# Odd layer of a two-block network: eight blocks of the output projection placed ahead of the last gate products

## The reference, cut to what matters

```python
def lru_direction(xc, w_a, b_a, w_x, b_x, lam, reverse):
    r = jax.nn.sigmoid((jnp.einsum('btnd,nde->btne', xb, w_a).reshape(B, T, W) + b_a).astype(jnp.float32))
    i = jax.nn.sigmoid((jnp.einsum('btnd,nde->btne', xb, w_x).reshape(B, T, W) + b_x).astype(jnp.float32))
    log_a = -LRU_C * r * jax.nn.softplus(-lam.astype(jnp.float32))
    a = jnp.exp(log_a)
    b = jnp.sqrt(-jnp.expm1(2.0 * log_a)) * i * xc.astype(jnp.float32)
    ...

def odd_layer(z, w_in, conv_w, conv_b, w_a, b_a, w_x, b_x, lam, w_out):
    zp = jnp.einsum('btd,de->bte', z, w_in)
    u, gate = split_cols(zp, ODD_SPLITS)
    ...
    y = (lru_direction(xc, w_a[0], b_a[0], w_x[0], b_x[0], lam[0], reverse=False)
         + lru_direction(xc, w_a[1], b_a[1], w_x[1], b_x[1], lam[1], reverse=True))
    y = y * jax.nn.silu(gate)
    return jnp.einsum('bte,ed->btd', y, w_out)
```

## Time and profile before

| what | value |
|---|---|
| median of 3 runs | 1892.74 us (1888.79 to 1895.13) |
| profiled execution | span 1893.4 us |
| TensorE busy | 1860.5 us, 98% of the span |
| VectorE, ScalarE, GpSimd busy | 606.7, 431.5 and 60.8 us |
| odd layer, from its first matmul on | 1687 to 1893 us of the span |
| output projection in the trace | 1833.4 to 1890.3 us |

### The profile page before, as it was taken

One profiled execution on the slowest core, in us unless ns is written; L12 is line 12 of the kernel. 1 busy time (PEld: TensorE's weight loads), 2 busy tenths in 40 slices (PEclk: granted clock), 3 DMA queues, 4 the chain that ended last, 5 costly groups with the idle time before them and its releaser, 6 DMA issues.

```text
span 1893.4 us, 20864 instructions
## 1 busy us (share of the span) xinstructions
PE 1860.5 (98%) x8529; PEld 1015.8 (54%) x8537; DVE 606.7 (32%) x1501; ACT 431.5 (23%) x954; POOL 60.8 (3%) x61
## 2 busy tenths in 40 slices
PE   9999999999999999999999999999999999999999
PEld 8888754443443433455444344433365657468864
DVE  3665433111110103135311111100434556424662
ACT  2322211100000101142110010000135434217760
POOL 0000000000000000000000000000010000001110
PEclk9999999999999999999999999999999999999999
DMA  9433459999999999416999999999731313231530
GB/s 385 193 131 141 156 203 375 424 427 428 429 428 429 428 429 426 179 54 252 398 422 430 427 430 427 427 429 428 332 114 45 134 45 134 107 121 40 222 122 34
DMA packets 42640, 529.40 MB, mean 280 GB/s; under 512 B 4592, under 2 KB 8208, under 8 KB 10544
## 3 DMA queue, kind: packets, MB, share of 16 engines
q1 hardware_dynamic: 39728, 515.39, 65.6%
q10 hardware_dynamic: 2816, 12.65, 1.7%
HBM read 523.80 MB, written 4.23 MB: 279 GB/s over the span
## 4 chain that ended last, share of the span: by engine, by line
PE 82%; DMA 7%; DVE 5%; issue 4%; ACT 2%; POOL 1%; ACTq 0%; DVEq 0%; POOLq 0%
PE ps L202 33%; PE ps L689 20%; PE ps L712 10%; PE ps L721 5%; PE ps L659 4%; DMA ring<-in_wu 3%; DMA ring<-in_wg 3%; PE ps L1355 1%; PE ps L654 1%; PE ps L571 1%; PE ps L698 1%; PE ps L497 1%; PE ps L988 1%; POOL small L2592 1%; PE ps L1137 0%
## 5 line engine op out<-in xcount | busy, mean ns | idle before, releaser
L689 PE MATMUL ps<-ring,work 128*64 128x512 f32 x1792 | 393.2, 593 | 3.3 <-DMA ring<-in_wu 1.8
L202 PE MATMUL ps<-xl,ring 128*128 128x256 f32 (+3 forms) x1344 | 292.3, 376 | 0.9 <-DVE xl L2305 0.9
L689 PEld LDWEIGHTS ps<-ring,work 128*64 128x64 f32 x1792 | 128.3, 137 | 260.1 <-issue 254.0
L202 PEld LDWEIGHTS ps<-xl,ring 128*128 128x128 f32 x1344 | 245.3, 191 | 40.3 <-issue 2.3
L202 PE MATMUL ps<-ring,xl 128*128 128x256 f32 (+2 forms) x672 | 202.8, 459 | 2.1 <-DVE work L2288 1.1
L712 PE MATMUL ps<-ring,work 128*64 128x512 f32 x896 | 199.3, 596 | 2.3 <-ACT work L1580 2.3
L202 PE MATMUL ps<-ring,big 128*128 128x512 f32 x448 | 197.9, 598 | 2.9 <-ACT ring L1859 2.4
L2153 DVE TENSOR_TENSOR work<-work,ps 128x512 f32<-128x512 f32 x32 | 22.0, 687 | 524.5 <-PE ps L689 524.5
L202 PEld LDWEIGHTS ps<-ring,xl 128*128 128x128 f32 x672 | 125.5, 190 | 70.1 <-issue 57.2
L202 PEld LDWEIGHTS ps<-ring,big 128*128 128x128 f32 x448 | 84.3, 191 | 105.2 <-issue 102.1
L712 PEld LDWEIGHTS ps<-ring,work 128*64 128x64 f32 x896 | 61.5, 137 | 117.5 <-issue 114.3
(11 more groups left out here) (374 smaller groups left out, 1671.3 us busy)
## 6 DMA issues: line engine op xcount, KB each, us to landing
ring<-in_wg SPq DMA_DIRECT2D x56, 2048.0 KB, 17.6
ring<-in_wu SPq DMA_DIRECT2D x56, 2048.0 KB, 20.5
ring<-in_wd SPq DMA_DIRECT2D x56, 2048.0 KB, 22.8
xl<-in_wg SPq DMA_DIRECT2D x8, 2048.0 KB, 17.4
xl<-in_wu SPq DMA_DIRECT2D x8, 2048.0 KB, 22.5
xl<-in_wd SPq DMA_DIRECT2D x8, 2048.0 KB, 27.0
ring<-in_w_odd SPq DMA_DIRECT2D x8, 2048.0 KB, 8.7
ring<-in_w_xz SPq DMA_DIRECT2D x7, 2048.0 KB, 17.0
```

Source lines behind the costliest of these rows:

```text
L202: i = e.matmul(bout, lhs(k), rhs(k), start=start and k == ks[0], stop=stop and k == ks[-1])
L689: last = e.matmul(b[64 * j:64 * j + 64, :], x[:, 4 * a + k, 64 * j:64 * j + 64], w[:, 4 * j + k, :], start=a + k == 0, stop=a + k == 4)
```

## The change

It has four parts.

1. The products of blocks 0 to 7 with the first column half (n = 0) are issued before the gate products of column block 7. Those with the second half (n = 1) are issued right behind these gate products. The blocks 8 to 13 and 14 to 15 follow in the order of before.
2. A bank for a sum is taken just before the sum's first product, and not all four at once. A new method `oldest` reduces the running index before it calls `hold`.
3. The sum of tile t = 1, n = 1 is made as two sums of 256 columns in two banks, so that five banks are held in place of four.
4. The last addition and the last store are cut in two accordingly. Five stores of 256, 256, 256, 128 and 128 KB are issued, and SP waits for 80 in place of 64.

The order of SP's loads and the slots of the ring stay as they are.

```diff
+    def oldest(self, key):
+        self.i %= len(self.banks)
+        return self.hold(key)
...
-        oo_mm = then(mm_cb, (0, 8), range(2), range(2))
+        OUT = ((0, 0, 0, 512), (0, 1, 0, 512), (1, 0, 0, 512), (1, 1, 0, 256), (1, 1, 256, 256))
+        oo_mm = Sig(mm_cb.sem, [(k, n, t, c) for k in (0, 8) for n, t, c, _ in OUT], mm_cb)
...
+        def tensor_odd_out(e, k0, k1, n):
+            c0 = k0 // 8 * 8
+            e.wait_ge(*ring("oo", c0, n))
+            if n == 0:
+                e.wait_ge(*y_in(k1 // 2 - 1))
+            wv = kview(8, 512)(ring.view("oo", c0, n))
+            for nn, t, c, w in OUT:
+                if nn != n:
+                    continue
+                if k0 == 0:
+                    b, gone = eb.oldest(("oo", n, t, c))
+                    if gone:
+                        e.wait_ge(*gone)
+                last = project(e, eb["oo", n, t, c][:, 0:w], lambda k: yT[:, k, 16 + t * 128:144 + t * 128],
+                               lambda k: wv[:, k - c0, c:c + w], range(k0, k1), start=k0 == 0, stop=k1 == 16)
+                if k0 != 8:
+                    last.then_inc(*oo_mm.up(c0, n, t, c))
...
             for cb in range(8):
+                if cb == 7:
+                    tensor_odd_out(e, 0, 8, 0)
                 tensor_odd_gates(e, cb)
                 if cb < 7:
                     tensor_odd_conv(e, cb + 1)
                     tensor_odd_gate(e, cb + 1)
-            for t in range(2):
-                for n in range(2):
-                    b, gone = eb.hold(("oo", t, n))
-                    if gone:
-                        e.wait_ge(*gone)
-            for k0, k1, ready in ((0, 8, 3), (8, 14, 6), (14, 16, 7)):
-                c0 = k0 // 8 * 8
+            tensor_odd_out(e, 0, 8, 1)
+            for k0, k1 in ((8, 14), (14, 16)):
                 for n in range(2):
-                    e.wait_ge(*ring("oo", c0, n))
...
+                    tensor_odd_out(e, k0, k1, n)
...
-            for n in range(2):
-                for t in range(2):
-                    e.wait_ge(*oo_in(n, t))
-                    e.dma_start(out[0, t * 128:t * 128 + 128, n * 512:(n + 1) * 512],
-                                h[:, t, n * 512:(n + 1) * 512]).then_inc(stored, 16)
+            for n, t, c, w in OUT:
+                e.wait_ge(*oo_in(n, t, c))
+                e.dma_start(out[0, t * 128:t * 128 + 128, n * 512 + c:n * 512 + c + w],
+                            h[:, t, n * 512 + c:n * 512 + c + w]).then_inc(stored, 16)
...
-            for n in range(2):
-                for t in range(2):
-                    hh = h[:, t, n * 512:(n + 1) * 512]
-                    e.wait_ge(*oo_mm(8, n, t))
-                    e.tensor_tensor(hh, hh, eb["oo", t, n][:, :], ALU.add).then_inc(*oo_in.up(n, t))
+            for n, t, c, w in OUT:
+                hh = h[:, t, n * 512 + c:n * 512 + c + w]
+                e.wait_ge(*oo_mm(8, n, t, c))
+                e.tensor_tensor(hh, hh, eb["oo", n, t, c][:, 0:w], ALU.add).then_inc(*oo_in.up(n, t, c))
...
-            e.wait_ge(stored, 64)
+            e.wait_ge(stored, 80)
```

More of the change, by code:

```diff
@@ L307, in build @@
         oc_mm, og_mm, lr_mm = then(mm_conv, G8, range(2)), then(mm_z, G8, range(2)), then(tr_x, G8, G8)
-        oo_mm = then(mm_cb, (0, 8), range(2), range(2))
+        OUT = ((0, 0, 0, 512), (0, 1, 0, 512), (1, 0, 0, 512), (1, 1, 0, 256), (1, 1, 256, 256))
+        oo_mm = Sig(mm_cb.sem, [(k, n, t, c) for k in (0, 8) for n, t, c, _ in OUT], mm_cb)
         oc_in, sq_in, b_in, y_in = then(conv, G8, range(2)), then(xd_in, G8), then(dec_d, G8), then(dec_in, G8)
-        oo_in = then(yv_in, range(2), range(2))
+        oo_in = Sig(yv_in.sem, [x[0:3] for x in OUT], yv_in)
         og_in, lr_in, lt_in = then(zs_in, G8, range(2)), then(mx_in, G8, G8), then(Bl_in, G8)
@@ L399, in build @@
             for n in range(2):
-                ring.add(("oo", k0, n), 1, oo_mm(k0, n, 1), E)
+                ring.add(("oo", k0, n), 1, oo_mm(k0, n, 1, 256 * n), E)
         ygT = area(big, 0, (16, 256))
@@ L1371, in tensor_odd @@
                     tensor_odd_gate(e, cb + 1)
-            for t in range(2):
+            tensor_odd_out(e, 0, 8, 1)
+            for k0, k1 in ((8, 14), (14, 16)):
                 for n in range(2):
-                    b, gone = eb.hold(("oo", t, n))
-                    if gone:
-                        e.wait_ge(*gone)
-            for k0, k1, ready in ((0, 8, 3), (8, 14, 6), (14, 16, 7)):
-                c0 = k0 // 8 * 8
-                for n in range(2):
-                    e.wait_ge(*ring("oo", c0, n))
-                    wv = kview(8, 512)(ring.view("oo", c0, n))
-                    for t in range(2):
[L1383 to L1388, removed]
+                    tensor_odd_out(e, k0, k1, n)
         def tensor(e):
```

## The result

The changed kernel takes 1900.99 us (median of 8 runs, 1897.54 to 1905.79), the kernel before on the same chips 1893.57 us (8 runs, 1888.79 to 1898.97). The ratio is 1.0042 with a 95% interval of 1.0030 to 1.0054: slower, by 0.42%, clear of the noise. The forecast was 1899.5 us.

The account below looks back on a forecast made before the run. TensorE was taken to bound the kernel. Terms -2.38 gap, -1.65 its clock, +8.94 new gap, +2.0 its clock, +0.1 banks, +0.09 split, -0.27 tail: 1892.7 + 6.8 = 1899.5 us, range 1896.0 to 1903.0.

Parts of the forecast that it names:

- The gap before and its clock: TensorE ahead of the projection: 2.38 us waiting for ScalarE's sigmoids plus 1.65 us at low clock, 4.0 us removable.
- The n = 0 block ahead of the gate products: TensorE before block 7's gate products: 32 records moved ahead, 13.73 us, without a wait.
- The banks: Gate products of block 7 with six banks rotating: the seventh product late, 0.1 us taken.
- The release of `oo(0,1)`: SP issues this `odd_out` load only behind block 7's gate products, at 1844.88, so its wait is uncovered.
- The landing: oo(0,1) lands 8.9 us after issue, so TensorE has a new gap of 8.94 us before the n = 1 products.
- the rival of a sooner landing: At TensorE's new gap: oo(0,1) lands 1.2 to 3.1 us sooner, 1898.3 to 1896.4 us; chance 0.12.
- The 6.8 us: Alternative estimate for landing oo(0,1): about 2.0 us fixed plus bytes over 436 GB/s; would give 1897.4 us.
- The clock: Behind TensorE's new gap the granted clock has fallen, costing 2.0 us.
- The rival with 5.1 us: Behind the new gap the clock stays low longer, up to 10.2 us: 5.1 us lost, 1902.6 us; chance 0.12.
- The split: The projection's t = 1, n = 1 sum as 64 records of 256 columns: costs 0.09 us.
- The tail: From TensorE's last product to the end: 2.87 us, 0.27 us less by the halved addition, nothing from the halved store.
- The other engines: ScalarE and VectorE work moved later: `y_in(6)` by 1858.6 at latest, covered by the new wait; uncovered, 0 to 0.3 us.

Follow-up runs that it names:

- e3: The kernel before with only the four banks taken one by one, oldest first, nothing moved and no sum cut: ratio 0.9983.
- e1: The changed kernel with lru1's slot passed over, so oo(0,1), oo(8,0) and oo(8,1) take slots free before the gate products: 1889.64 us, ratio 0.9979.
- e5: The changed kernel with the products of blocks 0 to 7 put back behind the gate products, banks singly and cut sum kept: 1889.09 us, ratio 0.9985.
- e4: The changed kernel with nine matmuls of no use ahead of the wait for oo(0,1): ratio 1.0030.
- e6: The changed kernel with oo(8,0) and oo(8,1) loaded first and oo(0,1) last, alone in flight, in lru1's slot: ratio 1.0038.
- e7: The changed kernel with lru1's slot passed over and both column halves of blocks 0 to 7 ahead of the gate products: ratio 1.0066.

## Why the prediction was right

- **The gap before and its clock** (4.0 us): right in size. e3 takes them away alone, 2.38 us and 1.77 us in place of 1.65. The reading "the four banks taken at once" is incomplete: which banks `hold` picked has by the code a part in it, as said at e3.
- **The n = 0 block ahead of the gate products** (13.73 us): right, 1841.87 - 1828.13 = 13.74 us.
- **The banks** (0.1 us): the gate products took 3.72 us as before, so it was nothing. The table load that I left open does come behind the wait: it began at 1842.57, after the first product, and the first sigmoid at 1843.86. The seventh product had its bank all the same.
- **The release of `oo(0,1)`**: right. SP issued at 1845.62; the forecast of 1844.88, moved by the 0.83 us of the part ahead, is 1845.71. e1 shows by one edit that this is the cause.
- **The landing** (8.9 us, gap 8.94): 8.5 and 8.54, so 0.4 us too much. The trace of before was the right row, and its own scatter is that large: 8.4 in e5, 8.2 in e4. The row of 7.7 us for `w_lru`, on which the rival of a sooner landing leant, did not come from another state of the queue: in the trace of before nothing moved from 1755 to 1760, and the load was issued at 1759.85 with three more behind it. Loads of `w_lru` were the faster ones in every trace (7.6 to 8.0 us), and no run shows why. The 6.8 us from the Trainium skill's "DMA: Bandwidth & Descriptors", section on the anatomy of one DMA, did not hold, in e6 neither, where the load had the queue for itself (8.4 us). That estimate, and the rival of a sooner landing, would have given a time too low.
- **The clock** (2.0 us): too low, the only term missed by much. It took 2.9 us (44.46 against 41.55 in e4). I had taken the value near the stretch behind the short gap; the longer gap had the longer stretch, 5.9 us of work. The rival with 5.1 us was right about the length of the low stretch, 10.2 us here too, but it counted all of it as work, and 4.3 us lay in the gap. In which part of the gap the clock falls is what both had left out.
- **The split** (0.09 us): 55.18 us in e5 against 55.10 in e3, so 0.08. The rest of the projection took 41.55 us in e4 against 27.46 + 13.82 + 0.30 = 41.58 in the sum.
- **The tail** (2.87 us): 1901.3 - 1898.6 = 2.7 us. The addition took 0.42 us as expected. The store of 128 KB landed in 1.8 us in place of 2.0, where I had expected no gain. The row of 64 KB on which I had put that (`xl<-in_meta`) is a load and not a store, so it bore on this term only loosely.
- **The other engines**: `y_in(6)` came at 1859.33 and was not waited for. The bound of 1858.6, moved by 0.83, was right to 0.1 us. Where the load doesn't cover it (e1) it costs 0.25 us, within the forecast's 0 to 0.3.

The errors of landing, banks and tail (-0.4, -0.1, -0.2) and that of the clock (+0.9) nearly cancel: +6.8 forecast, +7.1 in the profiles, +7.4 between the medians. The mechanism was read from the rows; that the sum came nearer than its terms is luck. Of the 1900.99 us, 0.8 also come from the median of before having moved from 1892.74 to 1893.57 with more runs.

## What to carry to other kernels

Before work is put ahead of other work on TensorE, read what hangs on the work that is put back: not only its readers, but also the ring slot that it frees, the load that waits for that slot, and the loads queued behind it. A load's cover is the work between its release and its first use; the change didn't add any waiting instruction to this load, it moved the cover to the wrong side. And the cheap part of a change should be tried alone: taking the oldest bank, one at a time, gave all of the gain that the reordering was to cover. Last, a running index into a list from which entries are removed no longer names the oldest one.

## What the runs showed of the hardware

- A load of `odd_out` (2 MB) into an idle queue landed after 8.2 to 8.9 us, whether two more were queued behind it (before 8.9, changed 8.5) or none (8.4 in e6, 8.6 to 8.7 for the three of e1). Loads of `w_lru`, as large, also into an idle queue, landed after 7.6 to 8.0 us; why they are faster stays open. The load of e6 moved 131 GB/s in the second microsecond and about 400 later, so size over the highest rate (4.8 us) and one empty microsecond fall short by 2.6 us.
- The granted clock's low level reached further into the work behind the long gaps: 3.4 us behind 2.38 us of idling, 5.9 us behind 8.54, 5.2 us behind 8.47 (e6, 1847.9 to 1853.1), 5.8 us behind 13.05 (e7). Behind the short gap it began 1.4 us after TensorE had resumed; behind the long ones it began within the gap (at 1849.8 in the changed kernel, 4.3 us before the work). It cost 1.7 us behind the short gap, 2.9 in the changed kernel and 2.5 in e6 (44.09 against 41.55). A gap of 0.60 us (e4) left the clock full. What sets the length was not tried.
- Halving the last store from 256 to 128 KB brought its landing from 2.0 to 1.8 us.
